# Differential attention: the scores of its first three row blocks are made inside the value projection

## The reference, cut to what matters

```python
proj = h @ w_in[l]
q_da, k_da, v_da, q_r, k_r, v_r, g_r, u_pool = jnp.split(proj, split_points, axis=-1)
o_da = diff_attention(q_da, k_da, v_da, ...)
...
s = jnp.einsum('bhmqd,bhmkd->bhmqk', q_blk, k).astype(jnp.float32) * scale
mask = kpos[None, :] <= qpos[:, None]
p = jax.nn.softmax(jnp.where(mask, s, -jnp.inf), axis=-1)
a = p[:, :, 0] - lam * p[:, :, 1]
return jnp.einsum('bhqk,bhkd->bhqd', a.astype(v.dtype), v)
```

## Time and profile before

| what | us |
|---|---|
| median of 3 runs (4076.68 to 4085.45) | 4079.43 |
| the profiled execution: its time | 4081.01 |
| the profiled execution: span of the trace | 4079.2 |
| PE busy in it | 3882.3 (95%) |
| DVE busy | 2207.4 (54%) |
| POOL busy | 1906.9 (47%) |
| ACT busy | 1436.9 (35%) |

### The profile page before, as it was taken

How to read it: one execution, slowest core, us unless ns; L and a number is a source line. 1 busy time by engine, 2 the same in 40 slices (tenths; PEclk the granted TensorE clock), 3 DMA queues, 4 the chain that set the end, 5 groups by cost and what they waited for, 6 DMA issues and landing times.

```text
span 4079.2 us, 49896 instructions
## 1 busy us (share of the span) xinstructions
PE 3882.3 (95%) x19191; PEld 3140.4 (77%) x19191; DVE 2207.4 (54%) x3488; ACT 1436.9 (35%) x2928; POOL 1906.9 (47%) x1707
## 2 busy tenths in 40 slices
PE   8999999999999999999898999999998898999998
PEld 4677788777888887786576788888786577788887
DVE  2242426482777775632637777624633638777633
ACT  1122223133666662222634333312222634333211
POOL 1313122272333334522234788986522135778975
PEclk9999999999999999999899999999998899999999
DMA  5312221232000003110022222453210033222543
GB/s 178 115 51 79 67 64 42 86 103 62 6 10 7 11 6 110 64 33 17 1 97 96 83 80 86 149 170 123 96 36 8 1 107 97 77 88 78 172 158 129
DMA packets 247508, 310.37 MB, mean 76 GB/s; under 512 B 38804, under 2 KB 161060, under 8 KB 247272
## 3 DMA queue, kind: packets, MB, share of 16 engines
q1 hardware_dynamic: 214456, 231.87, 18.5%
q10 hardware_dynamic: 32816, 75.32, 5.3%
HBM read 253.48 MB, written 51.53 MB: 75 GB/s over the span
## 4 chain that ended last, share of the span: by engine, by line
PE 73%; DVE 16%; ACT 4%; issue 4%; POOL 2%; DMA 1%; ACTq 0%; SPq 0%; DVEq 0%; POOLq 0%
PE ps L130 69%; PE ps L133 4%; DVE cst_sm L153 3%; DVE ml_p L142 3%; ACT thi L136 2%; DVE da_sg L159 1%; POOL wlo L142 1%; DVE tlo L142 1%; DVE f_ta L150 1%; DVE f_tb L150 1%; ACT ml_o L136 1%; ACT tfi L136 0%; POOL whi L139 0%; DVE tfl L142 0%; POOL mlo_z L142 0%
## 5 line engine op out<-in xcount | busy, mean ns | idle before, releaser
L139 POOL CAST whi<-wst 128x512 fp32r<-128x512 f32 (+3 forms) x524 | 424.5, 810 | 1429.8 <-DMA wst<-in_a_w_in 457.7
L142 POOL TENSOR_TENSOR wlo<-wst,whi 128x512 fp32r<-128x512 f32 (+2 forms) x650 | 926.8, 1433 | 42.1
L130 PE MATMUL ps<-whi,thi 128*128 128x512 f32 (+3 forms) x1816 | 707.5, 390 | 19.8 <-POOL wlo L142 6.0
L130 PE MATMUL ps<-whi,tlo 128*128 128x512 f32 (+3 forms) x1816 | 685.2, 377 | 0.0
L130 PE MATMUL ps<-wlo,thi 128*128 128x512 f32 (+3 forms) x1816 | 684.2, 377 | 0.0
L130 PEld LDWEIGHTS ps<-whi,thi 128*128 128x128 f32 x1816 | 344.5, 190 | 102.6 <-issue 25.6
L130 PEld LDWEIGHTS ps<-wlo,thi 128*128 128x128 f32 x1816 | 344.7, 190 | 58.1 <-issue 3.8
L130 PEld LDWEIGHTS ps<-whi,tlo 128*128 128x128 f32 x1816 | 343.7, 189 | 57.5
L130 PE MATMUL ps<-thi,whi 128*128 128x512 f32 x856 | 339.4, 397 | 15.7 <-POOL wlo L142 10.9
L130 PE MATMUL ps<-tlo,whi 128*128 128x512 f32 x856 | 337.8, 395 | 0.0
L130 PE MATMUL ps<-thi,wlo 128*128 128x512 f32 x856 | 337.3, 394 | 0.0
(11 more groups left out here) (389 smaller groups left out, 8244.6 us busy)
## 6 DMA issues: line engine op xcount, KB each, us to landing
wst<-in_w_down SPq DMA_DIRECT2D x140, 256.0 KB, 3.2
wst<-in_w_up SPq DMA_DIRECT2D x126, 256.0 KB, 3.0
scr_h<-f_tb SPq DMA_DIRECT2D x44, 512.0 KB, 4.0
wst<-in_w_in SPq DMA_DIRECT2D x64, 256.0 KB, 2.7
wst<-in_a_w_in SPq DMA_DIRECT2D x72, 192.0 KB, 2.4
wst<-in_ada_w SPq DMA_DIRECT2D x48, 256.0 KB, 3.4
da_am<-in_ada_w SPq DMA_DIRECT2D x48, 256.0 KB, 2.7
f_T2lw<-scr_h SPq DMA_DIRECT2D x48, 256.0 KB, 3.8
```

The source lines that it names most:

```text
L130: return self.none if self.e is None else self.e.matmul(*a, **k)
L139: return self.none if self.e is None else self.e.tensor_copy(*a)
L142: return self.none if self.e is None else self.e.tensor_tensor(*a)
```

## The change

- The scores of units 0, 1 and 2 (head 0, row blocks 7, 6 and 5) are moved out of the loop into the second group of the value projection, ahead of its weight blocks k = 2, 4 and 6 (`FIRST_UNITS`). Their exponentials are moved in `act_mix` ahead of the read-out of that group. DVE's instructions keep their order, and their maxima are now made while the projection runs. The loops of PE and ACT start at unit 3.
- The second group of the value projection takes banks 4 to 7 (`tr4`), so that banks 0 to 3 are free for the scores.
- The slot counter is padded before the value weights until `wn % 11` is 9, so that they lie in slots 9, 10 and 0 to 5 and leave `p2` free in time. Each of the first three exponentials waits for the projection's last use of `tlo` block i.
- DVE's clearing of `pw`, `wa`, `wb` moves from before unit 0 to step 3, and the scaling of `sgm` from step 2 to step 7.
- `WINDOWS` moves from steps 5, 6, 11, 12 to steps 8, 9, 15, 16.

```diff
-                B.take((st, it), ring)
+                B.take((st, it), ring if isinstance(ring, str) else ring[g])
@@ sp_mix
+            while n == 2 and self.wn % NS != 9:
+                self.wn += 1
@@ pe_mix
+                if n == 2 and b and k in self.FIRST_UNITS:
+                    self.pe_scores(q, l, self.FIRST_UNITS[k])
...
-            self.pe_tiles(q, ("c", l, n), 8, items, (3, 3, 2) if n == 3 and l == 0 else 4, "proj", terms, lambda k: ("c", l, n, k),
+            self.pe_tiles(q, ("c", l, n), 8, items, (3, 3, 2) if n == 3 and l == 0 else 4,
+                          ("proj", "tr4") if n == 2 else "proj", terms, lambda k: ("c", l, n, k),
@@ act_mix
+                if n == 2 and b:
+                    for i in range(3):
+                        self.act_exp(q, l, i)
...
-    WINDOWS = {1: (0, None), 5: (0, 0), 6: (0, 1), 7: (1, None), 11: (1, 0), 12: (1, 1)}
+    WINDOWS = {8: (0, 0), 9: (0, 1), 15: (1, 0), 16: (1, 1)}
@@ pe_diff, act_diff
-        for i in range(32 + 4):
+        for i in range(3, 32 + 4):
+    FIRST_UNITS = {2: 0, 4: 1, 6: 2}
@@ act_exp
+            if mp == 0:
+                if i >= 4:
+                    q.wait_ge(*S.at("turned", ("cT", l, i - 4, self.UNITS[i - 4][1] // 4)))
+                else:
+                    q.wait_ge(*S.at("tile", ("w", ("c", l, 2, i))))
@@ dve_diff
-        q.wait_ge(*S.at("tile", (("c", l, 2), 7)))
-        q.memset(self.pw[:], 0.0).then_inc(*S.up("pw_zero", l))
-        q.memset(self.wa[:, 0:16], 0.0)
-        q.memset(self.wb[:, 0:16], 0.0).then_inc(*S.up("mix_zero", l))
...
-            if i == 2:
+            if i == 3:
+                q.wait_ge(*S.at("tile", (("c", l, 2), 7)))
+                q.memset(self.pw[:], 0.0).then_inc(*S.up("pw_zero", l))
+                q.memset(self.wa[:, 0:16], 0.0)
+                q.memset(self.wb[:, 0:16], 0.0).then_inc(*S.up("mix_zero", l))
+            if i == 7:
```

More of the change, by code:

```diff
@@ L2398, in pe_diff @@
         S, B, ps = self.S, self.B, self.ps
-        q.wait_ge(*S.at("mask"))
-        for i in range(32 + 4):
+        for i in range(3, 32 + 4):
             if i < 32:
-                h, j = self.UNITS[i]
-                w = 128 * (j + 1)
-                bs = [B.take(("cs", l, i, mp), "s2") for mp in range(2)]
-                q.wait_ge(*B.done(("ct", l, "q", 7)))
-                q.wait_ge(*B.done(("ct", l, "k", 7)))
-                for c in range(0, w, 512):
-                    n = min(512, w - c)
-                    for mp in range(2):
-                        if c == 0:
-                            for event in B.freed(("cs", l, i, mp)):
-                                q.wait_ge(*event)
-                        r = slice(64 * mp, 64 * mp + 64)
-                        q.matmul(ps[:, bs[mp] + c // 512, 0:n], self.cq[r, h, blk(j)], self.ck[r, h, c:c + n], start=True,
-                                 stop=(c + n < w), skip_group_check=True)
-                for mp in range(2):
-                    q.matmul(ps[:, bs[mp] + c // 512, n - 128:n], self.idb[:], self.cmask[:], start=False, stop=True,
-                             skip_group_check=True).then_inc(*S.up("qk", ("c", l, i, mp)))
-            if i in self.WINDOWS and self.WINDOWS[i][1] is not None:
+                self.pe_scores(q, l, i)
+            if i in self.WINDOWS:
                 self.pe_window(q, l, *self.WINDOWS[i])
@@ L2444, in pe_diff, with pe_scores @@
             self.pe_diff_turn(q, l, h, "tr4")
+    FIRST_UNITS = {2: 0, 4: 1, 6: 2}
+    def pe_scores(self, q, l, i):
+        S, B, ps = self.S, self.B, self.ps
+        q.wait_ge(*S.at("mask"))
+        h, j = self.UNITS[i]
+        w = 128 * (j + 1)
+        bs = [B.take(("cs", l, i, mp), "s2") for mp in range(2)]
+        q.wait_ge(*B.done(("ct", l, "q", 7)))
+        q.wait_ge(*B.done(("ct", l, "k", 7)))
+        for c in range(0, w, 512):
+            n = min(512, w - c)
+            for mp in range(2):
+                if c == 0:
+                    for event in B.freed(("cs", l, i, mp)):
+                        q.wait_ge(*event)
+                r = slice(64 * mp, 64 * mp + 64)
+                q.matmul(ps[:, bs[mp] + c // 512, 0:n], self.cq[r, h, blk(j)], self.ck[r, h, c:c + n], start=True,
+                         stop=(c + n < w), skip_group_check=True)
+        for mp in range(2):
+            q.matmul(ps[:, bs[mp] + c // 512, n - 128:n], self.idb[:], self.cmask[:], start=False, stop=True,
+                     skip_group_check=True).then_inc(*S.up("qk", ("c", l, i, mp)))
     def pe_diff_turn(self, q, l, h, ring):
@@ L2511, in act_diff, with act_exp @@
             self.act_diff_hi(q, l, h)
+    def act_exp(self, q, l, i):
+        S, B, ps = self.S, self.B, self.ps
+        w = 128 * (self.UNITS[i][1] + 1)
+        for mp in range(2):
+            key = ("cs", l, i, mp)
+            b = B.of(key)
+            q.wait_ge(*S.at("c_max", (l, i, mp)))
+            if mp == 0:
[3 more added lines that the diff above has]
+                    q.wait_ge(*S.at("tile", ("w", ("c", l, 2, i))))
+            elif i >= 2:
+                q.wait_ge(*S.at("c_mix", (l, i - 2)))
+            dst = self.p1[i % 4] if mp == 0 else self.p2[i % 2]
+            q.activation(dst[:, 0:w], ps[:, b:b + 2, :].rearrange("p a b -> p (a b)")[:, 0:w], ACT.Exp,
+                         bias=self.cstat(i, 2 + mp), accum_out=self.cstat(i, 4 + mp)).then_inc(*B.free(key, "exp"))
     def act_diff_hi(self, q, l, h):
```

16 lines of the change are left out of this document (removed).

## The result

| | before | after |
|---|---|---|
| median, us | 4078.05 (4 runs) | 4043.45 (4 runs, 4036.9 to 4045.24) |
| ratio to before | | 0.991 [0.9898, 0.9922] |
| the profiled execution, us | 4081.01 | 4043.51 |

The account below looks back on a forecast made before the run. PE, with 73% of the chain that ended last, was taken as the bound. Gains of 11.3 us (layer 0) and 12.3 us (layer 1) took 4081.0 to 4057.4, less 1.6 for the median: 4055.8 us, range 4043 to 4073.

Parts of the forecast that it names:

- POOL's first stretch: POOL's work now beside units 3 to 6: charged 3.5 us a layer, bounds 0 and 9.2 us.
- steps 8 and later: Loop from unit 8: pool mixer 1.6 us, POOL's and the retention scaling's move 2.0 us; 3.6 us given back a layer.
- What leaves the path: Loop start, last value matmul to unit 3's scores: 18.5 us removed in layer 0, 18.0 us in layer 1.
- The inserts: Three units' scores inside the value projection's second group: cost 6.6 us a layer, bounds 5.7 and 8.3 us.
- Units 3 to 7: Loop behind the projection: 20.4 us including POOL's charge, a gain of 3.0 us in layer 0, 4.5 in layer 1.
- The 2.0 us for POOL's move: POOL's second stretch and the retention's scaling move from units 7-12 to 9-15: 2.0 us a layer (-1 to +6).
- more is gained: POOL's first stretch hides, clock stays up through head 0, pool mixer free at steps 8 and 9: 4041 us; chance 0.15.
- POOL and DVE block each other on narrow units: Some eight narrow units under POOL's work pay 3 us each; with half of them hit, 4070 us; chance 0.17.
- The ring is longer than two weight blocks: Inserted scores in the value projection wait some 2 us three times a layer, 12 us lost: 4068 us; chance 0.06.
- the clock falls inside the projection: Half-array scores or a PE wait bring the value projection to 1.2 GHz: 21.8 us a layer, 4099 us; chance 0.05.
- The change does not do what it says: Unit 3 waits for something late, such as ACT's value read-out; start-up partly paid again: 4076 us; chance 0.03.
- At no cost: Slot padding before the value weights, small tables' DMAs and the new wait on `tlo` were taken as free.

## What of the prediction held, and which step failed

**The step that failed** is the price of the conflicts behind the start-up, two terms of the sum. For POOL's first stretch beside units 3 to 7 I charged 3.5 us a layer, and it cost 1.5. For steps 8 and later I gave back 3.6 us a layer, and the runs show 1.0 and 0.0. Together that is 2 x 2.0 + 2.6 + 3.6 = 10.2 of the 13.9 us that were missed. The new places of the pool mixer show the same fault by themselves: worth 1.1 us a layer in my sum, 4.1 and 6.3 by the steps of the kernel that has them alone.

**What leaves the path** was right: the start-up is gone, and the fillers in the kernel before show that up to unit 3 it was 15.4 us of bare ring (0.6 of them a wait for banks) and some 3 us of low clock.

**The inserts** cost 5.9 us and not 6.6: the way from the read-out to the next scores behind the group grew from 23.86 us (1875.60 to 1899.46) to 29.75. The scores and masks are 2.02 + 1.80 + 1.58 = 5.4 us; stopping and resuming the stream take 0.17 us an insert (the scores start 0.32 us behind the last projection matmul and the second one behind them 0.31 us after the first, where the usual distance is 0.23), and not the 0.3 that I added. The Trainium skill (TensorEngine Tiling (Array Packing), Key Properties) says that a change of the tiling mode drains the engine. By these rows such a drain can be no more than the 0.17 us for the two changes of an insert; the trace neither needs it nor excludes it. This term gave 0.7 us in layer 0 and 0.8 in layer 1.

**Units 3 to 7** took 17.7 us, not 20.4. Two terms were too large. The steps without POOL sum to 3.35 + 4.60 + 3.29 + 2.74 + 2.20 = 16.2 and not 16.9 (unit 7 meets exactly the 2.20 us of unit 15). And POOL's first stretch costs 1.5 us, not the 3.5 that I charged "near the 3.1 us that unit 7 paid". POOL did fall on units 4 to 6 (1909.73 to 1920.41), and DVE's small operation did take 1.69 us as foretold; but only one step of the five grew, and there the maxima of the next unit have some slack. This gave 2.7 us a layer.

**Steps 8 and later**, step by step (us; steps that are missing here did not change by more than 0.01):

| step of unit | before, l0 / l1 | after, l0 / l1 | longer by, l0 / l1 |
|---|---|---|---|
| 8 | 6.12 / 5.05 | 4.70 / 4.70 | -1.42 / -0.35 |
| 10 | 4.79 / 5.91 | 7.67 / 7.66 | 2.88 / 1.75 |
| 11 | 6.02 / 6.69 | 5.44 / 5.77 | -0.58 / -0.92 |
| 12 | 4.80 / 5.14 | 5.59 / 5.27 | 0.79 / 0.13 |
| 13 | 4.83 / 4.83 | 3.29 / 3.29 | -1.54 / -1.54 |
| 15 | 2.20 / 2.20 | 3.11 / 3.11 | 0.91 / 0.91 |

The first two places of the pool mixer cost less than the 1.6 us that I charged: nothing at step 8 (4.70 us, as unit 16 took without one), and some 1.1 us of the step from unit 10, behind the mixer at step 9 (5.90 us without POOL; 4.79 in the kernel with this place at step 12, where neither stands there). "Even" for the move from 11 and 12 to 15 and 16 was wrong: step 13 loses 1.5 us, and step 15 takes on only 0.9. The 2.0 us for POOL's move cannot be set against one number. In after, POOL's second stretch costs 3.3 and 3.7 us at units 10 to 12. But it no longer stands on units 7 and 8, where step 8 took 0.35 us more than now at clock 1.00, and 1.4 more at clock 0.72 in layer 0, behind a wait of PE of 2.79 us in step 7 (1937.91 to 1940.70). What it cost at units 9 to 12 of the kernel before, no run tells.

Together: 0.7 + 0.8 from the inserts, 2 x 2.7 from units 3 to 7, 2.6 + 3.6 from units 8 to 15, 0.4 + 0.8 behind them (the clock at the wide units, which varies by up to 3 us between kernels with the same code there), less 0.5 between the layers: 13.8 of the 13.9 us that were missed.

**The common fault** is one of method. I priced each conflict by how far DVE's instruction would be stretched, or by the one step that paid most, and not by what PE's steps would lose. The inserts, POOL's first stretch and the first two places of the mixer came out below the value that I took, and so did the whole of steps 8 and later. With all four unknown costs at their lower bounds (0.9 + 3.5 + 1.6 + 3.0 us a layer) my own sum would have been 4038; the range stopped at 4043. The case "more is gained" names the same causes; it deserved more than 0.15, and the range should have held all of it. That the median is still inside the range, by 0.45 us, is luck.

**The rivals.** "POOL and DVE block each other on narrow units" did not happen as a whole: POOL's second stretch lies beside units 9 to 15 and costs at three steps of them, 10 to 12. It is a true mechanism, though: the run with the mixer at narrow units pays 3.3 us at step 13 behind two stretched instructions of DVE. The Trainium skill (GPSIMD Engine Reference, Specifications) states that GpSimd and VectorE share SBUF interfaces, with contention for VectorE instructions that have two SBUF inputs. The traces agree: 0.22 us become 1.69 and 1.28 become 3.00 beside POOL. "The ring is longer than two weight blocks" and "the clock falls inside the projection" did not happen either (no wait at the inserts, clock 1.00). "The change does not do what it says" was wrong for three inserts; with four, the late read-out is there, at 0.74 us.

**At no cost** held for banks and padding (0.9996). It left one thing out: the order of POOL and the pool mixer. I had treated the new places as a minor cost; by the medians they are worth 13 us alone and 22 us under the inserts.

## What to carry to other kernels

Independent short work that starts a dependent loop can be put into a matmul stream that bounds the stage before it; it costs its PE time and little more, and it takes away both the bare ring and the low clock behind it. When the loop starts earlier, everything that was timed against its steps (another engine's table, a mixer that reads it) has to move later by as much. Price a conflict between engines by what the next wait on the bounding engine grows, read from the steps, and not by what the stretched instruction grows.

## What the runs showed of the hardware

- Useless matmuls in PE's waits kept the granted clock at 1.00 also where the waits were short and the clock only partly low: 21.30 us at 0.76 became 19.20 us. The fillers pay for themselves there, if nothing else needs the bank that they write.
- A DVE instruction of one column takes 0.22 us alone and up to 1.86 us beside POOL; a mix of 128 columns 0.35 alone and 2.52, one of 1024 columns 1.28 and 3.00. The addition is as large for a narrow operation as for a wide one, because it is a wait: all 164 one-column instructions that lasted over 0.3 us ended 0.01 to 0.02 us behind the end of a POOL operation. The two maxima of 768 columns, which read PSUM, do not stretch (1.82 us together alone, 1.81 beside POOL's 3.20 us operation at 1937.85).
- Stopping a stream of full-array matmuls for half-array ones and going on cost 0.17 us at clock 1.00 (distances of 0.32 and 0.31 us between starts instead of 0.23).
